# Block 1's attention: the low parts of every other weight piece are made by GpSimd instead of VectorE

## The reference

```python
for l in range(DEPTH):                       # 2 layers, T = 16 + 512 tokens
    hn = rms_norm(h, norm_mix_g[l])
    proj = hn @ w_in[l]
    q, k, v, xr, gate = jnp.split(proj, splits, axis=-1)
    ...
    q = apply_partial_rope(rms_norm(q, q_norm_g[l]), cos, sin)
    k = apply_partial_rope(rms_norm(k, k_norm_g[l]), cos, sin)
    o_attn = diff_attention(q, k, v, lam)    # softmax(1) - lam * softmax(2), 4 heads
    o_attn = (rms_norm(o_attn, subln_g[l]) * (1.0 - lam_init)).reshape(B, T, D_ATTN)
    o_rec = rg_lru_branch(xr, gate, ...)     # conv, gates, scan over time
    h = h + jnp.concatenate([o_attn, rms_norm(o_rec, ...)], axis=-1) @ w_out[l]
    ...
```

## Time and profile before

| what | value |
|---|---|
| median of 3 runs | 2864.66 us (2860.75 to 2864.87) |
| the profiled execution's own time | 2860.26 us |
| its span in the trace | 2858.5 us |
| PE busy | 2768.6 us, 97% |
| DVE busy | 1651.1 us, 58% |
| ACT busy | 1268.0 us, 44% |
| POOL busy | 370.8 us, 13% |
| L1757 (all low parts) | 446 instructions, 557.5 us, 1251 ns each |

### The profile page before, as it was taken

How to read it: one execution, slowest core, us unless ns; L and a number is a source line. 1 busy time by engine, 2 the same in 40 slices (tenths; PEclk the granted TensorE clock), 3 DMA queues, 4 the chain that set the end, 5 groups by cost and what they waited for, 6 DMA issues and landing times.

```text
span 2858.5 us, 39044 instructions
## 1 busy us (share of the span) xinstructions
PE 2768.6 (97%) x15748; PEld 2346.3 (82%) x15752; DVE 1651.1 (58%) x2479; ACT 1268.0 (44%) x2133; POOL 370.8 (13%) x291
## 2 busy tenths in 40 slices
PE   8999999999989999999999999999999999999997
PEld 7878999999877788887668888888776688888886
DVE  6786545454777745454876466333658764653335
ACT  5574322224674422233564545333445644443333
POOL 2222000001222000000223120000312231200003
PEclk9999999999999999999999999999999999999999
DMA  4112232232112233332123223323221232233332
GB/s 145 52 45 67 89 91 90 94 90 83 51 45 74 93 96 97 102 94 88 56 75 126 89 67 96 98 94 97 84 81 61 77 126 82 67 104 96 95 97 67
DMA packets 71923, 244.36 MB, mean 85 GB/s; under 512 B 9152, under 2 KB 10816, under 8 KB 71744
## 3 DMA queue, kind: packets, MB, share of 16 engines
q1 hardware_dynamic: 66528, 235.50, 25.7%
q10 hardware_dynamic: 5216, 6.36, 0.7%
HBM read 239.73 MB, written 2.10 MB: 85 GB/s over the span
## 4 chain that ended last, share of the span: by engine, by line
PE 83%; DVE 11%; ACT 3%; issue 2%; POOL 0%; DMA 0%; SPq 0%; ACTq 0%; DVEq 0%
PE psum L578 23%; PE psum L584 23%; PE psum L581 23%; PE psum L650 2%; DVE temp L2194 1%; DVE weights_hi_lo L1757 1%; PE psum L1080 1%; PE psum L673 1%; PE psum L675 1%; PE psum L1092 1%; PE psum L677 1%; DVE small L2192 1%; PE psum L907 1%; PE psum L935 1%; PE psum L960 1%
## 5 line engine op out<-in xcount | busy, mean ns | idle before, releaser
L578 PE MATMUL psum<-act_hi_lo,weights_hi_lo 128*128 128x264 f32 (+2 forms) x2544 | 776.3, 344 | 3.7 <-ACT temp L1290 2.8
L581 PE MATMUL psum<-act_hi_lo,weights_hi_lo 128*128 128x264 f32 (+2 forms) x2544 | 750.9, 334 | 1.9 <-DVE weights_hi_lo L1757 1.9
L584 PE MATMUL psum<-act_hi_lo,weights_hi_lo 128*128 128x264 f32 (+2 forms) x2544 | 752.1, 335 | 0.0
L1181 ACT ACTIVATE weights_hi_lo<-weights_float 128x1024 fp32r<-128x1024 f32 (+2 forms) x446 | 463.7, 1042 | 499.1 <-PE psum L584 430.7
L1757 DVE TENSOR_TENSOR weights_hi_lo<-weights_float,weights_hi_lo 128x1024 fp32r<-128x1024 f32 (+2 forms) x446 | 557.5, 1251 | 219.4 <-ACT weights_hi_lo L1181 218.1
L578 PE MATMUL psum<-hidden_hi_lo,weights_hi_lo 128*128 128x512 f32 (+2 forms) x1584 | 519.6, 358 | 3.7 <-DVE x_residual L2010 1.4
L584 PE MATMUL psum<-hidden_hi_lo,weights_hi_lo 128*128 128x512 f32 (+2 forms) x1584 | 511.6, 353 | 1.4 <-DVE hidden_hi_lo L2020 1.4
L581 PE MATMUL psum<-hidden_hi_lo,weights_hi_lo 128*128 128x512 f32 (+2 forms) x1584 | 511.2, 352 | 1.3 <-DVE weights_hi_lo L1757 1.3
L578 PEld LDWEIGHTS psum<-act_hi_lo,weights_hi_lo 128*128 128x128 f32 x2544 | 439.7, 189 | 68.3 <-issue 17.7
L584 PEld LDWEIGHTS psum<-act_hi_lo,weights_hi_lo 128*128 128x128 f32 x2544 | 438.4, 188 | 48.1
L581 PEld LDWEIGHTS psum<-act_hi_lo,weights_hi_lo 128*128 128x128 f32 x2544 | 438.0, 188 | 47.9 <-issue 2.6
(11 more groups left out here) (290 smaller groups left out, 3297.5 us busy)
## 6 DMA issues: line engine op xcount, KB each, us to landing
weights_float<-in_w_ff SPq DMA_DIRECT2D x128, 512.0 KB, 3.6
weights_float<-in_w_gu SPq DMA_DIRECT2D x88, 512.0 KB, 3.6
weights_float<-in_w_in SPq DMA_DIRECT2D x70, 512.0 KB, 3.6
weights_float<-in_w_down SPq DMA_DIRECT2D x32, 448.0 KB, 3.3
weights_float<-in_w_out SPq DMA_DIRECT2D x16, 512.0 KB, 3.6
weights_float<-in_w_down SPq DMA_DIRECT2D x16, 512.0 KB, 3.5
weights_float<-in_w_mv SPq DMA_DIRECT2D x16, 512.0 KB, 3.2
weights_float<-in_w_mix SPq DMA_DIRECT2D x16, 512.0 KB, 3.3
```

The costliest lines, as they stand in the source:

```text
L578: e.matmul(slot[:, place:place + c1 - c0], w_hi[:, col], x_hi[:, c0:c1], start=first, stop=False)
L581: e.matmul(slot[:, place:place + c1 - c0], w_lo[:, col], x_hi[:, c0:c1], start=False, stop=False)
L584: mm = e.matmul(slot[:, place:place + c1 - c0], w_hi[:, col], x_lo[:, c0:c1], start=False, stop=final)
L1181: e.activation(K.parts(n)[0][:, 0:cols], K.staged(n)[:, 0:cols], ACT.Copy).then_inc(*K.did("hi", n))
```

## The change

POOL gets the low part of six pieces a layer, at the steps 21, 29, ..., 61, and DVE no longer makes these. The work, its operands and the buffers stay the same. The low parts made by POOL count on a semaphore of their own, `lo_pool`; PE and SP wait for whichever engine made the piece.

```diff
+POOL_SPLIT = {s: 6 + s // 4 for s in range(21, 4 * len(ORDER1), 8)}
+POOL_PIECES = {PIECE["w_v", _l, 0] + ahead for _l in range(DEPTH) for ahead in POOL_SPLIT.values()}
...
+    def low(self, n):
+        return self.done("lo_pool" if n in POOL_PIECES else "lo", n)
...
-    w.wait_ge(*K.done("lo", n))
+    w.wait_ge(*K.low(n))
...
-def split_lo(e, w, K, n):
+def split_lo(e, w, K, n, name="lo"):
...
         e.tensor_tensor(lo[:, 0:cols], K.staged(n)[:, 0:cols], hi[:, 0:cols].bitcast(F32), ALU.subtract).then_inc(
-            *K.did("lo", n))
+            *K.did(name, n))
...
-        if s % 4 == 1 and s < 4 * len(ORDER1):
+        if s % 4 == 1 and s < 4 * len(ORDER1) and s not in POOL_SPLIT:
             split_lo(e, w, K, first + 4 + s // 4 + 2)
...
+        if s in POOL_SPLIT:
+            split_lo(e, w, K, PIECE["w_v", l, 0] + POOL_SPLIT[s], "lo_pool")
         if s - 3 in STAT_AT1:
```

More of the change, by code:

```diff
@@ L2634, in load @@
             w.wait_ge(*done("hi", n - STAGING))
-            w.wait_ge(*done("lo", n - STAGING))
+            w.wait_ge(*K.low(n - STAGING))
         src = K.piece(n)
```

## The result

| what | before | after |
|---|---|---|
| median, same chip | 2861.03 us (2859.14 to 2864.87, 6 runs) | 2871.89 us (2869.15 to 2874.71, 6 runs) |
| profiled execution, its time and span | 2860.26, 2858.5 us | 2874.68, 2872.8 us |
| granted TensorE clock, mean of its span | 0.995 | 0.994 |

The ratio is 1.0032 [1.0021, 1.0043]: the change makes the kernel 9.2 us slower (6 to 12), where 7.6 was forecast. One execution of the change in a later comparison took 12791 us and one of the kernel before 9143 us, for a reason that nothing on record shows, and they stand in no ratio and in no median given here.

What follows compares the result with a forecast made beforehand. PE was taken to bound the kernel, with 83% of the chain that ended last. Costs of 4.4 us at E and 3.2 at C sum to 7.6; on the median of 2864.66 that gives 2872.3, forecast 2872, range 2864 to 2877.

Steps and rivals of the forecast that it cites:

- C: Step 37 of each layer: combination L1981 ends 2.2 us later, PE's reserve is 0.60; cost 2 x 1.6 = 3.2 us.
- E: Step 53 of each layer: convolution and L1960 come 2.2 us later, PE already waits; cost 2 x 2.2 = 4.4 us.
- GpSimd's row: The moved 128x1024 subtraction on GpSimd: estimated between 2.20 and 2.52 us, taken at 2.4.
- The row from which 4.4 would have followed: Rival: GpSimd's row is dear, doubled from a 128x512 subtraction of 2.22 us; 2880 to 2886, at 3 us about 2876; chance 0.10.
- The hold: DVE rows with two SBUF inputs kept out by GpSimd's subtraction: 2.2 us, ends 2.0 and 2.5.
- The reserve of 0.60 us: At C: L1981 ends at 136.15, PE's transposes L833 start at 136.75; PE has 0.60 us before it waits.
- The places costed at nothing: A, B, D and F: delays on DVE or GpSimd covered by savings or existing waits; cost 0.
- A: Step 21: convolution held some 1.2 us, cancelled by the 1.13 us saved behind it; cost nothing.
- B: Step 29: L2536 ends by 113.1, ACT's L1300 cannot run before 113.61, so 0.5 us covers it; cost nothing.
- F: Step 61: DVE's scan and rows behind come 1.1 us later; a 1.33 us wait for PE absorbs it; cost nothing.
- D: Step 45: DVE at most 1.1 us later, covered by PE's 1.70 us wait for ACT's exponential; cost nothing.
- The freed 13.6 us of DVE: 1.13 us saved per subtraction, six a layer; rival that it wins: 2851 to 2859 us, chance 0.04.

Runs made afterwards that it cites:

- E alone: Changed kernel with only place E (step 53) of each layer on GpSimd: 2866.81 us, ratio 1.0012 against before.
- C alone: Changed kernel with only place C (step 37) of each layer on GpSimd: 2865.54 us, ratio 1.0005 against before.
- the pair: Changed kernel with only places C and E (steps 37 and 53) of each layer on GpSimd: 2872.42 us, ratio 1.0036 against before.
- the fills: Changed kernel, at C and E GpSimd fills the low part with zeros three times instead of subtracting: 2863.66 us, ratio 0.9999 against before.
- the move behind: Changed kernel, all twelve on GpSimd, waiting at C for DVE's combination and at E for its convolution to end: 2862.88 us, ratio 0.9997 against before.
- the change again: The changed kernel unaltered, timed again beside three follow-up kernels: 2873.26 us, ratio 1.0033 against before.
- the subtraction twice: Changed kernel, GpSimd makes the same low part twice at C and E, the other places on DVE: 2885.12 us, ratio 1.0077 against before.
- the one-input product: Changed kernel, at C and E GpSimd multiplies the staged piece by zero instead of subtracting: 2865.48 us, one execution.

## Why the prediction was right

**Direction, places and mechanism.** All of it lies at C and E, twice each; the other places cost nothing measurable; GpSimd's read keeps DVE's two-input rows out; PE waits for the row behind them. E and C alone, the pair, the fills and the move behind show these separately, by their waits; the times of single places are too close to noise to do it.

**GpSimd's row** was taken at 2.4 us and is 2.35 to 2.40 where free. The row from which 4.4 would have followed was indeed no guide.

**The hold** was taken at 2.2 us and is 2.18 at C and 2.0 at E. At E it is less since GpSimd enters in between two rows, and the hand-over seems to cost less there than at a start together; that is a reading of two places, not a test.

**E**: 2.2 a layer forecast, 2.0 measured. **C**: 1.6 forecast, 1.5 measured. The reserve of 0.60 us read from two starts was therefore nearly right: 2.18 - 1.49 = 0.69. The expected waits were 2.7, 3.1 and 1.6; they are 2.47, 2.90 and 1.49.

**The places costed at nothing.** At A the convolution is held as foreseen and B's L2547 ends in time, as these rows of the profile after show, and at F DVE's held row is followed by a scan with no wait of PE for it. DVE's wait for PE behind it, named as F's cover, is 0.74 us where it was 1.33:

```profile
87.10 3.52 DVE L1933 SCALAR_TENSOR_TENSOR temp<-arena,params,temp 128x527 f32<-128x527 f32 x3
...
111.42 1.53 POOL L2547 TENSOR_SCALAR temp<-temp 128x528 f32<-128x528 f32 x1
...
174.23 0.66 PE L842 MATMUL psum<-consts,arena 128*128 128x128 f32 x4 [0.24 <-DVE arena L1898]
...
211.83 2.85 DVE L1952 SCALAR_TENSOR_TENSOR temp<-temp 128x528 f32<-128x528 f32 x1
214.60 1.25 DVE L1948 TENSOR_TENSOR_SCAN arena<-arena,temp 128x528 f32<-128x528 f32 x1
```

The third row is the one exception. The prediction gave D's cover as PE's wait for the exponential, and that wait does cover the rows there (1.44 us where it was 1.70), but DVE is still a little late six microseconds further on, where L842 waits 0.24 us. The term "nothing" at D should have read 0.2 a layer, 0.4 in all.

**The freed 13.6 us of DVE** are worth nothing, as forecast, and the run without the twelve subtractions measures it by itself.

**The sum.** 7.6 us forecast; by waits 7.0 and 0.4 for D, 7.4; by time 9.2 in the first comparison, 9.4 in that of the change again and 10.3 in that of the pair (ratios 1.0033 and 1.0036 of 2863), each to within 3 to 4 us. So 7.4 lies inside every interval, but all three measured values lie above it.

**The time of 2872** is met to 0.1 us, and that is luck. It was 7.6 on top of the median of 2864.66 of three executions; in the comparison the kernel before had 2861.03, 3.6 less, and the medians lie 10.9 us apart, 3.3 more than 7.6. The two cancel.

**The clock.** The term that the sum lacks is the granted clock. Averaged over the timed runs, it is 0.9947 or 0.9948 for before in the three later comparisons (for the first, only that of the profiled execution is on record). A clock lower by d costs about d x 2870 us:

| kernel | clock, against before | clock's share, us | stalls, us | sum | measured by ratio |
|---|---|---|---|---|---|
| E alone | 0.9952, 0.9947 | -1.4 | 4.0 | 2.6 | 3.4 |
| C alone | 0.9950, 0.9947 | -0.9 | 3.0 | 2.1 | 1.4 |
| the change again | 0.9942, 0.9947 | 1.4 | 7.4 | 8.8 | 9.4 |
| C and E | 0.9940, 0.9947 | 2.0 | 7.0 | 9.0 | 10.3 |
| the subtraction twice | 0.9926, 0.9948 | 6.3 | 14.8 | 21.1 | 22.1 |

The stalls of the last row are 7.0 + 2 x (1.95 + 1.96). Each execution's clock is on record to three digits. Stalls and clock together come within 1.3 us of every measured value, and the clock makes up 4.3 of the 5.5 us by which the pair exceeds the sum of the two places alone. In the first comparison the change averaged 0.9947, no lower than before elsewhere, so the 1.8 us by which it lies above the stalls there is not the clock's by this measure. For the doubled subtraction the clock is needed to close the sum; for the change itself its share is within what the measurement can tell.

What lowers it was not settled. In eight cases (two layers of four traces) PE waited 2.47 to 2.91 us for L1969, and in five of them the L659 row behind it took 1.36 to 2.13 us instead of 1.16; with waits of 0.47 to 0.91 us, in before and five other kernels, it took 1.16 in all twelve, and so it did behind the 1.13 and 1.55 us of the one-input product. That speaks for the long wait as a trigger. Three things keep it from being shown. E alone has the same waits and on average a higher clock than before. The clock also falls elsewhere in kernels without any new wait: in before around 225 and 870 us, and in the kernel without the twelve subtractions at four places of the two attention stages, at an unchanged time. And the loss by windows over the whole span, 13.2 us in before, is 9.9 us in the trace of the subtractions behind DVE's rows and 17.0 in that without them, neither of which has a longer wait at C or E. No run made PE wait at E for 2.5 us for another reason than DVE.

## What to carry to other kernels

Before a row with two SBUF inputs moves from VectorE to GpSimd, look at what VectorE does in the moment when GpSimd may start, not at how full either is: here GpSimd got in between two back-to-back rows, and most of its row (2.0 to 2.18 of 2.38 us) was paid by whatever stood behind. Behind the row that TensorE waits for it cost nothing that could be measured; but ask first what the freed VectorE time is worth, by a run that leaves the work out, since here it was nothing and the best placement could only equal the kernel before. The time lost lay 1.8 to 7.3 us above the stalls where both places were held and 0.6 to 1.6 us below them where one was, in part by the granted clock, so such a forecast needs a margin of its own for that.

## What the runs showed of the hardware beyond expectation

- GpSimd's two-input 128x1024 subtraction keeps DVE's two-input rows out for 2.0 to 2.18 of its 2.38 us; a one-input product of the same size, itself longer at 2.78, for 0.65 to 0.84; a fill of the same size (0.95 to 0.99 us each) for nothing. The Trainium skill, in SBUF — State Buffer, section SBUF: two separate sides, has the first to start hold the shared pair for the whole instruction; the two-input rows agree with that (2.18 of 2.39), the one-input row doesn't (0.84 of 2.78), and there the measurement decides.
- The one-input product takes longer on GpSimd (2.78 us) than the subtraction with two inputs (2.38), both started at the same point beside the same DVE rows. Whether it was itself held in between can't be told from the row.
- Behind a wait of 2.47 to 2.91 us, PE's next row ran in part at the lower clock in 5 of 8 cases, and behind those of 3.44 to 4.86 us of the doubled subtraction in 3 of 4.
